# One-core transformer block: the nets' inner rows stored, loaded back and split at later units of the same order

## What is computed

```
g, u = split(x @ w_gu)            # 1024 -> 2 x 2816
out  = (silu(g) * u) @ w_down     # 2816 -> 1024
```

## Time and profile before

| | |
|---|---|
| median of 3 runs | 891.3 us (890.01 to 892.44) |
| the profiled execution | 890.65 us, of which the span of the profile is 888.9 us |
| PE busy | 878.5 us, 99% of the span |
| DVE busy | 631.6 us, 71% |
| ACT busy | 460.7 us, 52% |
| moved by DMA | 215.12 MB, mean 242 GB/s |
| weight loads of the nets' way up | 130 of 512 KB, median 5.6 us to landing |
| `inner_rows` stores / loads | 60 of 128 KB, median 3.8 us / 15 of 512 KB, 5.2 us (and a smaller set for q = 5) |

### The profile page before, as it was taken

How to read it: one execution, slowest core, us unless ns; L and a number is a source line. 1 busy time by engine, 2 the same in 40 slices (tenths; PEclk the granted TensorE clock), 3 DMA queues, 4 the chain that set the end, 5 groups by cost and what they waited for, 6 DMA issues and landing times.

```text
span 888.9 us, 11084 instructions
## 1 busy us (share of the span) xinstructions
PE 878.5 (99%) x4079; PEld 732.8 (82%) x4079; DVE 631.6 (71%) x883; ACT 460.7 (52%) x697; POOL 40.8 (5%) x66
## 2 busy tenths in 40 slices
PE   9999999999999999999999999999999999999996
PEld 7878888888998888888888888888888888888885
DVE  6769987837558877688578886875768766665743
ACT  6546554626688475446535554454445344444530
POOL 0010000022103000000000000001000100000000
PEclk9999999999999999999999999999999999999998
DMA  9899999774654454454699999975755577777741
GB/s 365 346 323 352 359 363 351 270 237 145 182 175 175 162 193 164 149 186 143 218 308 348 344 329 323 333 257 163 257 179 177 182 248 241 240 233 246 250 120 47
DMA packets 94879, 215.12 MB, mean 242 GB/s; under 512 B 14520, under 2 KB 46185, under 8 KB 94697
## 3 DMA queue, kind: packets, MB, share of 16 engines
q1 hardware_dynamic: 94104, 212.97, 69.8%
q10 hardware_dynamic: 720, 1.44, 0.4%
HBM read 204.66 MB, written 9.72 MB: 241 GB/s over the span
## 4 chain that ended last, share of the span: by engine, by line
PE 94%; DMA 2%; DVE 1%; issue 1%; ACT 1%; SPq 0%; POOL 0%; POOLq 0%; DVEq 0%
PE ps L741 29%; PE ps L743 29%; PE ps L742 29%; DMA t_raw<-in_f_up 2%; PE ps L679 1%; PE ps L656 1%; PE ps L649 1%; PE ps L858 1%; PE ps L874 1%; PE ps L816 0%; PE ps L850 0%; PE ps L798 0%; DVE t_wl L1209 0%; DMA t_acc<-in_xT 0%; PE ps L865 0%
## 5 line engine op out<-in xcount | busy, mean ns | idle before, releaser
L1209 DVE TENSOR_TENSOR t_wl<-t_raw,t_wh 128x1024 fp32r<-128x1024 f32 (+3 forms) x308 | 360.4, 1203 | 103.3 <-ACT t_wh L916 102.4
L916 ACT ACTIVATE t_wh<-t_raw 128x1024 fp32r<-128x1024 f32 (+3 forms) x308 | 307.8, 1040 | 106.9 <-DMA t_raw<-in_f_up 63.3
L741 PE MATMUL ps<-t_wh,t_XH 128*128 128x512 f32 (+2 forms) x640 | 250.2, 391 | 1.3 <-DVE t_wl L1209 1.3
L743 PE MATMUL ps<-t_wh,t_XL 128*128 128x512 f32 (+2 forms) x640 | 247.1, 386 | 0.0
L742 PE MATMUL ps<-t_wl,t_XH 128*128 128x512 f32 (+2 forms) x640 | 246.8, 386 | 0.0
L741 PEld LDWEIGHTS ps<-t_wh,t_XH 128*128 128x128 f32 x640 | 120.2, 188 | 24.8 <-DVE t_wl L1209 2.1
L743 PEld LDWEIGHTS ps<-t_wh,t_XL 128*128 128x128 f32 x640 | 120.1, 188 | 24.0
L742 PEld LDWEIGHTS ps<-t_wl,t_XH 128*128 128x128 f32 x640 | 120.3, 188 | 22.9
L741 PE MATMUL ps<-t_wh,t_YH 128*128 128x512 f32 x288 | 113.1, 393 | 0.2 <-DVE t_YL L1634 0.2
L743 PE MATMUL ps<-t_wh,t_YL 128*128 128x512 f32 x288 | 112.2, 390 | 0.0
L742 PE MATMUL ps<-t_wl,t_YH 128*128 128x512 f32 x288 | 112.2, 389 | 0.0
(11 more groups left out here) (225 smaller groups left out, 614.1 us busy)
## 6 DMA issues: line engine op xcount, KB each, us to landing
t_raw<-in_f_up SPq DMA_DIRECT2D x130, 512.0 KB, 5.6
t_raw<-in_f_dn SPq DMA_DIRECT2D x66, 512.0 KB, 5.5
t_raw<-in_ada SPq DMA_DIRECT2D x48, 512.0 KB, 6.3
inner_rows<-t_tp SPq DMA_DIRECT2D x60, 128.0 KB, 3.8
t_tp<-inner_rows SPq DMA_DIRECT2D x15, 512.0 KB, 5.2
t_raw<-in_mkv SPq DMA_DIRECT2D x8, 512.0 KB, 3.6
t_raw<-in_ga SPq DMA_DIRECT2D x8, 512.0 KB, 3.3
t_raw<-in_gc SPq DMA_DIRECT2D x8, 512.0 KB, 3.2
```

The costliest lines, as they stand in the source:

```text
L741: pe.matmul(o, xh, h, start=k == 0, stop=False)
L743: x = pe.matmul(o, xl, h, start=False, stop=k == n - 1)
L916: act.activation(wh[:, m % SPL, lo:w], raw[:, n % RAW, lo:w], ACT.Copy).then_inc(hi_made, 1)
L1209: dve.tensor_tensor(wl[:, n % RAW, lo:w], raw[:, n % RAW, lo:w], wh[:, m % SPL, lo:w].bitcast(F32), ALU.subtract).then_inc(drained, 1)
```

## The change

One line of `inner` in `schedule`:

```diff
-            ways = (3, 4, 6) if (f, q) == ("f1", 0) else (0, 1, 3 if q == 4 else 4)
+            ways = (3, 5, 7) if (f, q) == ("f1", 0) else (1, 2, 3) if q == 4 else (2, 4, 6)
```

## The result

| | before | after |
|---|---|---|
| median of 20 runs each, in turn | 890.52 us (889.79 to 892.64) | 891.99 us (891.14 to 894.30) |
| ratio after / before | | 1.0016, 95% interval 1.0009 to 1.0024 |
| span of the profile | 888.9 us | 889.9 us |
| PE waits for a split weight tile | 1.3 us in 2 pieces | 2.6 us in 3 pieces |

The change makes the kernel 1.5 us slower. That is under the 0.3% that I had called noise, but twenty runs of each resolve it, and it has the other sign than my -0.2 us. The distance to my 891.1 us is only 0.9 us, in part by luck: the kernel before came out at 890.52 us here, where I had reckoned from 891.3.

What follows compares the result with a forecast made beforehand. PE was taken to bound the kernel (busy 878.5 of 888.9 us). Terms -1.9 + 1.5 + 0.2 = -0.2 us against 890.65 gave 890.4; with the median 0.65 above that execution, 891.1 us, range 889.0 to 894.4.

Steps and rivals of the forecast that it cites:

- What bounds the kernel: Whole kernel: PE bounds it, busy 878.5 of 888.9 us; SP's 70 us of waits lie nearly all beside PE's work.
- Term 2: Block 4, second net: store and reload one unit down, reload 2.7 us later, lead 1.2 us; PE waits 1.5 us.
- Term 4: Block 4, third net: lead 4.6 us against a shift of one unit, 2.7 us; no loss.
- Term 3: Block 4, first net: store to reload 6.3 instead of 4.0 us, lead 2.1 us; loss 0.2 us, bounds 0 and 2.5.
- Term 1: Block 0, first net: loads of units 19 and 20 go ahead of the reload, ending PE's loss there; gain 1.9 us.
- The sum: Whole kernel: -1.9 + 1.5 + 0.2 = -0.2 us against the profiled execution's 890.65 us; forecast median 891.1 us, chance 0.45.
- The rule: DMA queues: descriptors are consumed in ring order, so reloads behind two weight loads pay for their bytes; not priced in the sum.
- rival 2: Block 4, first and second nets: reloads behind weight loads take 6.7 us each, losing 2.5 and 2.9 us; 894.8 us, chance 0.15.
- The signs I named: Profile after: PE idle near 57 us under 0.5, SP's transpose waits below 10, ACT's idle before second net's block-4 `inner` about 8.

Runs made afterwards that it cites:

- the second session: The unaltered change measured once more against the kernel before, five rounds beside the best version on one chip: 893.66 us, ratio 1.0030 (1.0018 to 1.0041).

## Why the prediction was wrong

- **What bounds the kernel: right.** PE is the bound, SP's 70 us of waits lie beside it, and taking away nearly 40 of them gained nothing by itself.
- **Term 2, block 4 of the second net, +1.5 us: right.** It measured 1.0 us idle, 1.3 with the slower start. The path was as told: the step stays, store and reload come a unit later, the lead of 1.2 us is used up. Two pieces were off in opposite directions: 5.5 us from store to reload instead of 6.3, and 5.6 instead of 5.3 from the reload to `inner`.
- **Term 4, the third net, nothing: right** in that PE doesn't wait.
- **Term 3, block 4 of the first net, +0.2 us: this step failed, by its size.** It measured 1.1 us idle, about 1.4 in all, the largest miss of the sum. The path was as told, and the 6.3 us from store to reload came as I had put them, though other profiles with this order have 5.2 to 6.4. Two pieces were wrong. I let the store begin "at the same time relative to PE", which is 5.4 us before unit 44; it began 4.9 us before it, as in every profile with block 4 at 1, 2, 3. And the reload took 4.9 instead of 4.45 us. So 0.5 + 2.3 + 0.5 - 2.1 (the lead) = 1.2 us of waiting, to which the slower start comes. With a lead of 2.1 us against a shift of 2.3, errors of half a microsecond were the whole term, and I should have given it a price for that.
- **Term 1, block 0 of the first net, -1.9 us: this step failed.** "I take the full gain" rested on unit 19 alone. Its wait did go. But I followed the loads on SP through the move, and not the `inner` step of the same block on ACT and DVE, which moved from in front of split 19 to in front of split 20. I also gave the reload's own place behind two loads no price: it took 5.65 us instead of 3.90 and came at 55.4, and split 20 was ready at 60.5 where PE wanted it at 59.9. So 0.5 us idle, about 0.8 in all, stay, and the gain is 1.1. By the estimate above, the step's new place alone would not have made this wait. The run with `inner` back in front of split 19 shows the mechanism at 3.2 us, the run with split 20 in front of `inner` takes it away. My own list of what moves said "one for block 0"; the sum did not use it.
- **The sum.** -1.1 + 1.3 + 1.4 = +1.6 us, where I had -0.2; the medians give +1.5. The direction was wrong because both misses were on the same side, and I took for no change what a longer measurement resolves. That the three pieces of one profile add up to the medians' difference is in part luck, as the same three stops came to 3.5 us idle in the second session instead of 2.6.
- **The rule.** I gave rival 2 (the reload behind weight loads) 0.15 with 6.7 us per reload. In the change's profile the reloads of block 4 took 4.9 and 5.6 us, so it hardly happened there: two loads had been issued 3.5 to 4 us ahead of each, as I had argued. In the second session's profile they took 6.1 and 5.7, and the time came nearer to that rival. The mechanism is real: at block 0, to which the rival gave no price, the reload went from 3.90 to 5.65 us, and with the reload issued right behind the loads it took 8.0.
- **The signs I named.** SP's waits for transposes fell to 4.5 us (under 10); ACT's idle time before `inner` in the second net grew to 7.75 us (I said about 8); between 60 and 120 us the only wait for `t_wl` is the one that ends at 60.59, of unit 20, which is block 0's and not DVE failing to hold its lead further on. "No idle time of PE near 57 us, or under 0.5 us" came true, and hid the step that failed: the idle time, 0.49 us, had moved on by a unit.

## What to carry to other kernels

When a wait on a transfer is moved in a hand-written order, list for every engine which step now stands right behind it, and compute that step's lead; time taken out of waits that were covered is worth nothing. If a wait can't come earlier, feed the work that doesn't depend on it in front of it, as far as its own inputs have landed and no further: here two splits one unit earlier turned +0.16% into -0.26%, and a third cost it all again. A transfer issued behind bulk loads on the same queue pays for those of their bytes that are still on the way, so moving loads ahead of it to fill a hole has a price.

## What the runs showed of the hardware that was not expected

- The same reload of 512 KB, issued within 0.25 us of the same moment, let ACT go on after 4.5 us or, with two fresh loads of 512 KB ahead of it on the queue, after 8.0 us. That is 3.5 us more, against the 2.7 us that the bytes alone would need at 392 GB/s. With the two loads issued 4.5 us ahead of it, at block 0, it was 5.65 instead of 3.90 us.
- The start of the kernel is not equally fast in every execution: the first store, at the same place in the order in all kernels, was issued at 38.75 us in one profile and at 39.30 in that of the kernel before, and as late as 39.97 in another, 1.2 us apart. A late start may make the leads behind it longer, so that part of it is taken back at the next wait; no run isolates that. Why it varies is open; PE's wait for the first high halves (`PE ps L679 <- ACT t_wh L951`) was 0.3 us in the change's profile and up to 0.9 us in others.
- A stop of PE costs more than its idle time: two stops with 1.3 us of it cost 1.9, and the change's three with 2.6 us cost about 3.5.
- With split 21 ahead as well, PE's wait of 2.1 us was followed by some 3.6 us at the lower clock (granted clock 0.62, then 0.52 of full), while waits of 2.1 us (the change again) and 3.2 us (`inner` in front of split 19) were not: there it stayed at 1.00.
